# Another order for the summed weight tiles of a hybrid decoder layer, with one copy on another engine and four loads at other places

## The reference

```python
o_a = merge_heads(fox_attention(q_a, k_a, v_a, log_f)).astype(x.dtype)
o_b = merge_heads(dilated_attention(q_b, k_b, v_b, slopes)).astype(x.dtype)
merged = jax.nn.sigmoid(ga) * (o_a @ w_br_fox[l]) + jax.nn.sigmoid(gb) * (o_b @ w_br_dil[l])
x = x + merged @ w_out[l]
```

## Time and profile before

| | |
|---|---|
| median of 3 runs | 1331.02 us (1330.96 to 1332.22) |
| the profiled execution's own time | 1332.22 us |
| its span, first to last instruction | 1330.4 us |
| TensorE busy | 1323.5 us, 99% |
| VectorE, ScalarE, GpSimd busy | 1155.3, 966.2, 175.4 us |
| granted TensorE clock | 1.0 over the whole span |

### The profile page before, as it was taken

One profiled execution on the slowest core, in us unless ns is written; L12 is line 12 of the kernel. 1 busy time (PEld: TensorE's weight loads), 2 busy tenths in 40 slices (PEclk: granted clock), 3 DMA queues, 4 the chain that ended last, 5 costly groups with the idle time before them and its releaser, 6 DMA issues.

```text
span 1330.4 us, 16581 instructions
## 1 busy us (share of the span) xinstructions
PE 1323.5 (99%) x6031; PEld 1096.5 (82%) x6031; DVE 1155.3 (87%) x1386; ACT 966.2 (73%) x1227; POOL 175.4 (13%) x193
## 2 busy tenths in 40 slices
PE   9999999999999999999999999999999999999998
PEld 7888888888888878888888888888888888888887
DVE  6868787888877878988689898999999999999998
ACT  6666666666665666667777878888888888888874
POOL 0121212021011020101010101111111102020200
PEclk9999999999999999999999999999999999999999
DMA  9877685758888797588879698999989899999996
GB/s 354 291 173 258 143 265 116 247 149 233 234 215 220 253 253 246 166 237 260 287 173 333 162 302 172 313 221 284 245 253 267 228 281 222 297 211 313 195 290 177
DMA packets 123442, 317.29 MB, mean 238 GB/s; under 512 B 12248, under 2 KB 13536, under 8 KB 123104
## 3 DMA queue, kind: packets, MB, share of 16 engines
q1 hardware_dynamic: 93008, 236.67, 51.0%
q0 software_dynamic: 25728, 75.51, 32.0%
q10 hardware_dynamic: 4624, 4.05, 1.0%
HBM read 314.08 MB, written 2.11 MB: 238 GB/s over the span
## 4 chain that ended last, share of the span: by engine, by line
PE 88%; DMA 6%; DVE 4%; ACT 1%; issue 0%; POOL 0%; SPq 0%; ACTq 0%
PE acc L939 12%; PE acc L943 12%; PE acc L941 11%; PE acc L977 9%; PE acc L981 9%; PE acc L979 9%; DVE w_lo L2242 3%; DMA raw_y<-w_in 2%; PE acc L1168 2%; PE acc L1164 2%; PE acc L1166 2%; PE acc L1143 2%; PE acc L1139 2%; PE acc L1141 2%; PE acc L1378 1%; DMA raw_x<-w_in 1%
## 5 line engine op out<-in xcount | busy, mean ns | idle before, releaser
L2242 DVE TENSOR_TENSOR w_lo<-raw,w_hi 128x1024 fp32r<-128x1024 f32 x224 | 271.0, 1219 | 58.1 <-ACT w_hi L1596 56.9
L1596 ACT ACTIVATE w_hi<-raw 128x1024 fp32r<-128x1024 f32 x224 | 233.7, 1054 | 74.6 <-PE acc L943 23.9
L939 PE MATMUL acc<-w_hi,actA 128*128 128x512 f32 x580 | 228.5, 394 | 0.0
L943 PE MATMUL acc<-w_hi,actA 128*128 128x512 f32 x580 | 226.2, 390 | 0.0
L941 PE MATMUL acc<-w_lo,actA 128*128 128x512 f32 x580 | 225.8, 389 | 0.0
L1596 ACT ACTIVATE w_hi<-raw_y 128x1024 fp32r<-128x1024 f32 x154 | 160.4, 1058 | 77.5 <-PE acc L943 23.0
L2242 DVE TENSOR_TENSOR w_lo<-raw_y,w_hi 128x1024 fp32r<-128x1024 f32 x154 | 185.2, 1219 | 21.1 <-ACT w_hi L1596 19.4
L2242 DVE TENSOR_TENSOR w_lo<-raw_x,w_hi 128x1024 fp32r<-128x1024 f32 x118 | 142.0, 1219 | 46.7 <-ACT w_hi L1596 46.6
L1596 ACT ACTIVATE w_hi<-raw_x 128x1024 fp32r<-128x1024 f32 x118 | 121.6, 1051 | 47.9 <-DMA raw_x<-w_in 21.0
L943 PEld LDWEIGHTS acc<-w_hi,actA 128*128 128x128 f32 x580 | 108.8, 188 | 23.1
L941 PEld LDWEIGHTS acc<-w_lo,actA 128*128 128x128 f32 x580 | 109.0, 188 | 21.9
(11 more groups left out here) (421 smaller groups left out, 2794.4 us busy)
## 6 DMA issues: line engine op xcount, KB each, us to landing
raw<-w_in SPq DMA_DIRECT2D x101, 512.0 KB, 4.7
raw<-w_down SPq DMA_DIRECT2D x59, 512.0 KB, 5.7
raw_x<-w_up SPq DMA_DIRECT2D x44, 512.0 KB, 4.9
raw_y<-w_up POOLq DMA_DIRECT2D x34, 512.0 KB, 7.6
raw_x<-w_in SPq DMA_DIRECT2D x28, 512.0 KB, 4.3
odd<-w_up SPq DMA_DIRECT2D x27, 512.0 KB, 5.1
work<-w_up SPq DMA_DIRECT2D x24, 512.0 KB, 5.5
work<-w_up POOLq DMA_DIRECT2D x24, 512.0 KB, 8.2
```

Source lines behind the costliest of these rows:

```text
L939: nc.tensor.matmul(o, lhsT=a_h, rhs=w_hi[:, s, k, :], start=first and k == 0, stop=False, skip_group_check=onto_seed)
L943: mm = nc.tensor.matmul(o, lhsT=a_l, rhs=w_hi[:, s, k, :], start=False, stop=last and k == KU - 1, skip_group_check=onto_seed)
L1596: nc.scalar.activation(w_hi[:, n % RING, :, :], src.rearrange("p (k n) -> p k n", k=KU), ACT.Copy).then_inc(hi_done, 1)
L2242: nc.vector.tensor_tensor(w_lo[:, n % RING, :, :], src.rearrange("p (k n) -> p k n", k=KU), w_hi[:, n % RING, :, :].bitcast(f32), ALU.subt ...
```

## The change

- The bases of the four sums are issued behind loads 4, 5, 6 and 7 in the order P4, P6, P7, P5, instead of behind 5, 6, 8 and 9 in the order P7, P6, P5, P4.
- GpSimd's adds are put in the order P4, P6, P7, P5, P4, P6, P4, and the two waits for `used` go.
- P7's copy out of bank 7 is done by VectorE instead of ScalarE, behind its conversion and low part in the step of unit Q,P7. Product P4 and `dil_gate` wait for it through `dil_rows`, and the counts of `dil_out` and `dil_rows` are renumbered.
- The four pair loads of `w_out` are issued behind loads 22, 23, 24 and 26 instead of 26 to 29.

```diff
-DIL_OUT = {"P1": 1, "P7": 2, "P6": 3, "P5": 4}
+DIL_OUT = {"P1": 1, "P6": 2, "P5": 3}
...
-PAIR_LOADS_AT = {26: (1, 0), 27: (1, 1), 28: (0, 0), 29: (0, 1)}
-DIL_BASE_AT = {5: "P7", 6: "P6", 8: "P5", 9: "P4"}
+PAIR_LOADS_AT = {22: (1, 0), 23: (1, 1), 24: (0, 0), 26: (0, 1)}
+DIL_BASE_AT = {4: "P4", 5: "P6", 6: "P7", 7: "P5"}
...
                 elif name == "P4":
-                    pe.wait_ge(dil_out, DIL_OUT["P7"])
+                    pe.wait_ge(dil_rows, 1)
...
-                elif name == "P7":
-                    nc.scalar.activation(dil_p7, bank[7], ACT.Copy).then_inc(dil_out, 1)
...
-                if unit[0] == "Q" and unit[1] in ("P1", "P7", "P6", "P5"):
+                if unit[0] == "Q" and unit[1] in ("P1", "P6", "P5"):
                     dil_copy(n, unit[1])
...
                 elif c == 1:
-                    dve.wait_ge(dil_out, DIL_OUT["P7"])
+                    dve.wait_ge(dil_rows, 1)
...
                 if c < 2:
-                    dve.wait_ge(dil_rows, c + 1)
+                    dve.wait_ge(dil_rows, c + 2)
...
                 if unit == ("Q", "P7"):
                     out_low(15)
+                    dve.wait_ge(used, BR_AT[unit] + 1)
+                    nc.vector.tensor_copy(dil_p7, bank[7]).then_inc(dil_rows, 1)
...
+            add_dil_tile("P4", 1)
+            add_dil_tile("P6", 1)
+            prepare_dil(13).then_inc(prep_ready, 1)
             add_dil_tile("P7", 1)
-            prepare_dil(13).then_inc(prep_ready, 1)
-            add_dil_tile("P6", 1)
-            pool.wait_ge(used, BR_AT["F", 1, 1] + 1)
             add_dil_tile("P5", 1)
+            add_dil_tile("P4", 2)
             prepare_dil(14).then_inc(prep_ready, 1)
             add_dil_tile("P6", 2)
-            pool.wait_ge(used, BR_AT["F", 1, 3] + 1)
-            add_dil_tile("P4", 1)
+            add_dil_tile("P4", 3)
             prepare_dil(15).then_inc(prep_ready, 1)
-            add_dil_tile("P4", 2)
-            add_dil_tile("P4", 3)
```

## The result

The changed kernel takes 1341.12 us (median of 6, 1340.17 to 1343.06) against 1332.01 us of the kernel before beside it on the chip (median of 6, 1330.96 to 1332.5): a ratio of 1.0074 [1.006, 1.0087], 9 us slower. The forecast was 1334.4 us, 3.4 us slower, in a range up to 1337.5 us. The direction is right, the size is not, and the time lies outside the range.

The account below looks back on a forecast made before the run. TensorE, busy 1323.5 of 1330.4 us, was taken as the bound. Sums +3.4, copy 0 and pair loads 0 on the profiled 1332.22 us gave 1335.6 us, or 1334.4 us from the median 1331.02 us; range 1330.5 to 1337.5 us.

Parts of the forecast that it names:

- the price of the sums: Branch stage, moved bases and adds: load 9 lands 3.4 us later, bounds 1.7 to 4.1, all reaching TensorE.
- the share, 0.60 of the lone rate: Branch stage DMA: beside GpSimd's adds, SyncE's queue keeps 58.7/98.3 = 0.60 of its lone rate.
- The start of the sharing: Branch stage DMA: first add active 1.20 us after issue, from 460.5 us before and about 459.0 us after.
- The ninth transfer: SyncE's queue: P4's base adds one transfer ahead of load 9's landing, nine for eight, 1.47 us each alone.
- Cost nothing: Earlier w_out loads: overtaken loads come one to two transfers later, covered by up to six units; cost nothing.
- without that cover: Earlier w_out loads: cost of 3 us if the units converted ahead of TensorE do not hide the later loads.
- Nothing gives it back later: After head 12: the 3.4 us delay is not recovered, TensorE being busy without a gap.
- Rival 4, the smaller share: Branch stage: beside steady adds SyncE's queue has 0.34 of its lone rate; load 9 6.1 us late, 1337.1 us; chance 0.13.
- P7's copy: Copy moved to VectorE: 0.68 us there, cost nothing with 0.3 us cover; without it 0.2 to 0.7 us.
- The signs that the prediction named: Head 12 wait near 5 us, load 9 over 13 us, first add 457 to 458, five before 473, no P4 wait.
- three signs of being wrong: Load 9 landing by 472 us, copy released by VectorE's softmax, or second TensorE wait at head 13 or product P4.
- The delay stays single: Head 13: its copy ends near 486 us, some 2.7 us ahead of TensorE, so no second wait.

Follow-up runs that it names:

- sums_only: Kernel before with only the bases' new places, the adds' new order and GpSimd's two waits removed: 1338.63 us, 1.0047.
- bases_only: Kernel before with only the four bases moved to their new places and order: 1332.35 us, 1.0008.
- bases_no_holds: Kernel before with the new bases and without GpSimd's two waits, adds in their old order, P7 first: 1332.23 us, 1.0002.
- pairs_only: Kernel before with only the four w_out loads moved up behind loads 22, 23, 24 and 26: 1334.64 us, 1.0025.
- adds_held: Changed kernel with GpSimd's first add waiting until TensorE has finished unit F,0,2: 1336.44 us, 1.0032 against the kernel before.
- holds_off: Kernel before with only GpSimd's two waits on TensorE removed, adds in their old order: 1335.25 us, 1.0014.
- copy_first: Kernel before with ScalarE's copy for head 12 moved ahead of load 9's conversion: 1331.4 us, 0.9993.
- held_and_back: Changed kernel with the first add held until unit F,0,2 is used and the w_out loads at their old places: 1333.81 us, 1.0008.
- both_first: Kernel before with head 12's copy ahead of load 9's conversion and head 13's softmax ahead of load 10 on both engines: 1332.68 us, 1.0002.
- order_with_holds: Kernel before with bases and adds in the new order, both GpSimd waits on TensorE kept: 1338.91 us, 1.0057.
- pairs_back: Changed kernel with the four w_out loads back behind loads 26 to 29: 1339.82 us, 1.0054 against the kernel before.
- copy_only: Kernel before with only P7's copy moved to VectorE: 1332.46 us, 1.0003.
- after_filled: Changed kernel with 28 more unused matmuls ahead of head 12's value product: 1339.29 us, 1.0053 against the kernel before.

## Why the prediction was wrong in size

1. **The step that failed first: the price of the sums.** The term was 3.4 us with bounds of 1.7 and 4.1; alone they cost 6.3 us (sums_only). The path was as described: load 9 late, its conversion late, the copy (L1608) behind it, TensorE at L1024. Load 9 was converted at 476.19 us, where the forecast had it landed at 474.5 and its upper bound at 475.2. What failed is the share, 0.60 of the lone rate as long as the adds run, read off before and carried over to the change. The 0.60 is the mean of one 5 us window of before, and in it the adds' queue almost stood still between P7's add and P6's (11 packets from 468 to 469 us). While both have packets, SyncE's queue keeps a third, and in the change it has that for 859 add packets ahead of load 9 instead of 390. The start of the sharing was wrong too, 1.2 us behind the issue where 4.3 us and more were measured, but alike in both kernels. The ninth transfer, the other half of the term, shows no price of its own: bases_only and bases_no_holds have it, and load 9 landed earlier than in before. The first add went out at 456.64 us, 0.9 us ahead of the time taken from load 5 and near that of the upper bound. All this is 5.1 us of wait. The other 1.5 us is the half clock behind the wait, for which the sum had no term at all; the profile of before, at 1.0 throughout, has no row for its price.
2. **The second step that failed: "Cost nothing" for the pair loads.** It cost 3 us by the ratio of pairs_only, the very 3 us that the prediction gave "without that cover" (in part by luck: those were two transfers, the profile has 2.68 us of wait and a half clock behind it). The cover was read off the ring: tiles are converted up to six units ahead of TensorE. But VectorE's program puts the merge, which TensorE needs now, behind a conversion that TensorE needs six units later, and that chain had 0.6 us to spare. It is the pattern of head 12 again, which the prediction described on ScalarE and did not look for on VectorE. "If a second wait of TensorE stands at head 13 or at product P4" named two wrong places for it. "Nothing gives it back later" holds, but more was taken.
3. **Rival 4, the smaller share,** gave 6.1 us for the sums, and 6.3 were measured. Its mechanism is the one that the traces show: one packet to one where both queues have packets (197 to 196 after, 133 to 129 in before, 272 to 272 in sums_only from 464 to 468 us). The Trainium skill's turn by turn service (DMA: Bandwidth & Descriptors, Queues, rings and completion order) agrees with these counts. That "the counts don't show them" read the 2.3 to 1 of the earlier trace rows, a mean over a pause, as a ratio of service; 428 to 306 and 499 to 236 after are such means too. That the rival came so near has luck in it: it let the sharing begin 3 us too early in both kernels, and its 6.1 us hold no half clock, where the measured 6.3 us do. Nor is its steady row of five adds the lever: adds_held has five in a row as well, but behind load 9, and 1.0 us of wait there. The lever is how many adds are served ahead of load 9.
4. **P7's copy** was right: 0.68 us on VectorE, no wait of TensorE, 1.0003.
5. **The signs that the prediction named** came at 456.64 us for the first add (forecast 457 to 458), with five adds out before 473 us, 15.0 us from issue to landing for load 9 (over 13), and no wait at product P4. The wait near 5 us was 6.7 us. None of its three signs of being wrong came, though it was wrong: they asked after another path, not after another size.
6. **"The delay stays single"** held for the heads: the profile of the change has no wait at head 13. In holds_off, copy_first, adds_held and held_and_back a wait of 1.5 to 2.1 us stands at head 13, in both_first one at head 14.

What stays open: the third wait of the profiled execution, 1.4 us at L1344. ScalarE's copy (L1964) came behind a conversion that stood 3.23 us for a tile of w_out. None of the other profiles has it at that size, so it may be this execution's own, and it may be why the profile's loss is 11.9 us and the median's 9. Open too is what holds head 12 for 1.0 to 2.0 us where load 9 is in time, and why order_with_holds lost more than its adds' packets account for.

## What to carry to other kernels

A cover is not how far ahead the tiles are converted, but how long before its use the last thing on that engine's in-order program ends; look behind every conversion that a moved DMA makes late for something that is wanted at once. Where two DMA queues share saturated engines, count what the second one gets served ahead of the tight load, not how many transfers it has in all, and take the share from a window in which both have packets throughout: delaying the first add until the tight loads are nearly through took 4.7 us off the changed kernel, with one line. And a wait of TensorE of several microseconds is to be priced with the half clock behind it.

## What the runs showed of the hardware that was not expected

- The granted clock fell to the 1.2 GHz level behind waits of 5.7 to 6.7 us in each profile that had one with TensorE idle. It cost 1.5 us on top in two (11.15 and, in sums_only, 11.08 us for a stretch that takes 9.61), but 2.5 us in pairs_back (12.10 us) and 2.8 us in order_with_holds (12.42 us, from 478.90 to 491.32 us). Around 2 us it mostly fell: 0.50 behind 1.98 us at L990 in the change, 2.06 us in holds_off, 1.96 us in bases_only, 1.95 us in copy_only, 2.3 us in adds_held, 2.68 us in pairs_only; 1.00 behind 1.9 us in after_filled, 1.69 us in adds_held and 1.63 us in before. So the profiled executions of bases_only and copy_only, 4.4 and 2.5 us over their medians, have a half clock in them, while most of their runs show a mean clock of 1.0.

```profile
478.90 1.22 PE L1024 MATMUL acc<-softmax,odd 128*128 128x256 f32 x2 [6.34 <-ACT softmax L1608]
...
491.32 0.49 PE L1017 MATMUL acc<-smalls_sb,softmax 128*128 128x128 f32 x3
```

- An add in the buffer costs the DMA engines about twice a plain load, packet for packet. From the 465 to 470 us rows after, 0.608 x 5 x 16/306 = 159 ns against 0.478 x 5 x 16/428 = 89 ns; before, 165 and 86 ns. It is so without the other queue as well: in adds_held from 469.5 to 471 us the adds were alone and moved 105 packets per us, against SyncE's 202 alone.

```profile
q0 software_dynamic: 158, 0.32, 115.9%
```

- Between the issue of an add and its first packet lay over 4 us (4.3 us in before, 4.5 us after), although GpSimd's instruction takes 1.20 us.
